# First modulation quarter in two eighths with three column groups in flight, and other orders on VectorE later on

## The reference, cut to what matters

```python
mod = jax.nn.silu(c) @ w_ada[l] + b_ada[l]
sh_m, sc_m, ga_m, sh_f, sc_f, ga_f = jnp.split(mod[:, None, :], N_MOD, axis=-1)
h = rmsnorm(x, g_pre_mix[l]) * (1.0 + sc_m) + sh_m
hq, hf, hi, hg, cq, ckv, kr, gate_a, gate_b = jnp.split(h @ w_in, split_idx, axis=-1)
...   # gated recurrence, latent attention, both projected; merged with sigmoid gates
x = x + ga_m * rmsnorm(y, g_post_mix[l])
h = rmsnorm(x, g_pre_ffn[l]) * (1.0 + sc_f) + sh_f
y = swiglu(h, w_gate_up[l], w_down[l])
x = x + ga_f * rmsnorm(y, g_post_ffn[l])
```

## Time and profile before

| what | value |
|---|---|
| median of the runs | 1868.36 us (1868.06, 1868.36, 2447.69) |
| the profiled execution's own time | 1869.41 us |
| its span | 1867.6 us |
| PE busy | 1820.3 us, 97% of the span |
| DVE busy | 1297.1 us, 69% |
| ACT busy | 894.0 us, 48% |
| moved by DMA | 423.38 MB, mean 227 GB/s |

### The profile page before, as it was taken

One profiled execution on the slowest core, in us unless ns is written; L12 is line 12 of the kernel. 1 busy time (PEld: TensorE's weight loads), 2 busy tenths in 40 slices (PEclk: granted clock), 3 DMA queues, 4 the chain that ended last, 5 costly groups with the idle time before them and its releaser, 6 DMA issues. The chain is left out here.

```text
span 1867.6 us, 24368 instructions
## 1 busy us (share of the span) xinstructions
PE 1820.3 (97%) x8828; PEld 1529.1 (82%) x8828; DVE 1297.1 (69%) x1373; ACT 894.0 (48%) x1023; POOL 105.1 (6%) x74
## 2 busy tenths in 40 slices
PE   3999999999999999999999999999999999999997
PEld 3878888888888888888888878888888888888886
DVE  6889768677677677668787555656666666665657
ACT  5544555645645645644444456443443443443343
POOL 0000000130130130130000000000000000000000
PEclk8999999999999999999999999999999999999999
DMA  9997547656656656547787645666666666665553
GB/s 360 402 385 270 190 169 279 227 175 220 226 175 218 230 171 219 202 158 244 282 324 242 225 158 193 221 231 221 206 235 225 212 224 225 224 212 176 195 188 128
DMA packets 115985, 423.38 MB, mean 227 GB/s; under 512 B 13008, under 2 KB 13392, under 8 KB 115408
## 3 DMA queue, kind: packets, MB, share of 16 engines
q1 hardware_dynamic: 115920, 422.51, 65.7%
HBM read 420.36 MB, written 2.10 MB: 226 GB/s over the span
## 5 line engine op out<-in xcount | busy, mean ns | idle before, releaser
L1320 DVE TENSOR_TENSOR wlo<-raw,whi 128x1024 fp32r<-128x1024 f32 x600 | 731.9, 1222 | 401.6 <-ACT whi L484 400.7
L484 ACT ACTIVATE whi<-raw 128x1024 fp32r<-128x1024 f32 x600 | 630.0, 1053 | 718.6 <-PE PS L898 660.4
L890 PE MATMUL PS<-whi,hT_hi 128*128 128x512 f32 x1760 | 694.4, 395 | 4.9 <-issue 3.0
L891 PE MATMUL PS<-whi,hT_lo 128*128 128x512 f32 x1760 | 686.5, 390 | 0.0
L898 PE MATMUL PS<-wlo,hT_hi 128*128 128x512 f32 x1760 | 471.4, 390 | 0.0
L890 PEld LDWEIGHTS PS<-whi,hT_hi 128*128 128x128 f32 x1760 | 331.2, 188 | 72.4 <-issue 3.3
L898 PEld LDWEIGHTS PS<-wlo,hT_hi 128*128 128x128 f32 x1760 | 330.8, 188 | 69.6
L891 PEld LDWEIGHTS PS<-whi,hT_lo 128*128 128x128 f32 x1760 | 331.3, 188 | 66.6 <-issue 0.2
L890 PE MATMUL PS<-whi,cT_hi 128*128 128x512 f32 (+1 forms) x592 | 229.4, 389 | 1.4 <-DVE side L1644 1.4
L891 PE MATMUL PS<-whi,cT_lo 128*128 128x512 f32 (+1 forms) x592 | 226.1, 384 | 0.0
L1327 DVE SCALAR_TENSOR_TENSOR ada_acc<-ada_raw,csilu,ada_acc 128x512 f32<-128x512 f32 (+1 forms) x185 | 141.2, 763 | 27.3 <-DMA ada_raw<-in_ada 23.4
(11 more groups left out here) (238 smaller groups left out, 1112.3 us busy)
## 6 DMA issues: line engine op xcount, KB each, us to landing
ada_raw<-in_ada SPq DMA_DIRECT2D x142, 512.0 KB, 4.8
raw<-in_w_gate SPq DMA_DIRECT2D x88, 512.0 KB, 4.1
raw<-in_w_up SPq DMA_DIRECT2D x88, 512.0 KB, 4.1
raw<-in_w_down SPq DMA_DIRECT2D x88, 512.0 KB, 4.1
raw<-in_w_start SPq DMA_DIRECT2D x80, 512.0 KB, 4.9
raw<-in_w_hf SPq DMA_DIRECT2D x32, 512.0 KB, 3.7
raw<-in_w_hq SPq DMA_DIRECT2D x32, 512.0 KB, 5.1
raw<-in_w_hi SPq DMA_DIRECT2D x32, 512.0 KB, 4.3
```

Of the source, the lines that this page charges most:

```text
L484: nc.scalar.activation(whi[:, pl.slot(c), 0:w], raw[:, pl.slot(c), 0:w], ACT.Copy)\
L890: nc.tensor.matmul(o, hi[:, kt, tok], whi[:, s, cols], start=c == 0 and k == 0, stop=False)
L891: nc.tensor.matmul(o, lo[:, kt, tok], whi[:, s, cols], start=False, stop=False)
L1320: nc.vector.tensor_tensor(wlo[:, s, 0:w], raw[:, s, 0:w], whi[:, s, 0:w].bitcast(F32), ALU.subtract)\
```

## The change

It has five parts.

1. **Eighths.** Slices 0 to 15 are cut otherwise on the host: the first eight hold all of the depth for the first eighth (256 rows of h, one chunk's depth), the next eight for the second. DVE takes each slice as two dependent instructions of 128x512 (`eighth_chunk`). Slices 1 and 3 are multiplied by PE (`shared_chunk`, 8 products with one column each), and PE's sum of the first eighth is laid on top.
2. **Three groups in flight.** With only the first eighth of h, PE multiplies the first chunk of groups 0, 1 and 2 (the third in banks 6 and 7), then the second chunk of each. The x transposes are spread between them.
3. **A later second quarter of modulation.** `ADA_PACE` takes 16 slices by chunk 19 instead of 15. For quarter 1 the sum moves behind the ninth group (ahead of chunk 18), the scale to chunk 20 on DVE, ACT's scaling to chunk 20, and the low part to chunk 21 on DVE. For quarters 2 and 3 these stand where they stood. `add_pair` goes ahead of the slice in DVE's loop.
4. **Later orders.** `T_OG` from 20 to 19. At the channel mixer's entry ACT takes `square_x2(0, ...)` ahead of `high(first, 1)`, and DVE takes each `h2_low` before the `low` or `mix_x2` that it followed.
5. **The end.** DVE no longer finishes token tile 0 before the last sums of tile 1: `add_rows(2, 1)` and `add_rows(3, 1)` stand between the output pieces of tile 0.

```diff
+ADA_SHARED = [1, 3]
+N_E = 3
-ADA_PACE = [(0, 0), (15, 16), (20, 21), (35, 32), (55, 48), (80, 48)]
+ADA_PACE = [(0, 0), (3, 2), (19, 16), (20, 17), (35, 32), (55, 48), (80, 48)]
...
+            return i * N_E + j if j < N_E else j * W_G + i
...
-            for a in range(KD):
+            for a in range(ADA_SLOTS):
                 load_ada0(a)
...
+            for c in range(N_E):
                 load(start, c, w_start[c])
+            for a in range(ADA_SLOTS, KD):
+                load_ada0(a)
+            load(start, N_E, w_start[N_E])
...
             high(pl, 0)
+            scale_rows(1, 0, 1)
             high(pl, 1)
-            scale_quarter(0)
+            copy_xT(2)
+            copy_xT(3)
+            high(pl, 2)
+            copy_xT(4)
+            copy_xT(5)
+            scale_rows(2, 1, 2)
+            copy_xT(6)
+            high(pl, N_E)
+            copy_xT(7)
...
-                if i == 17 and n < PH - 1:
-                    scale_quarter(n + 1)
+                for q, at in ((1, SG * W_G), (2, 2 * SG * W_G - 3), (3, 3 * SG * W_G - 3)):
+                    if c == at:
+                        scale_rows(q + 2, q * KP_Q, (q + 1) * KP_Q)
...
+            for a in ADA_SHARED:
+                shared_chunk(a)
+            pe.wait_ge(sig("constants_loaded"), 16)
+            pe.wait_ge(sig("x_scaled"), TT)
+            transpose_x(0)
+            transpose_x(1)
+            sum_first_eighth()
...
+            first_tile(0, 0)
+            transpose_x(4)
+            pe.wait_ge(sig("xT_copied"), 4)
+            first_tile(1, 0)
+            transpose_x(5)
+            first_tile(2, 0)
+            sum_second_eighth()
+            transpose_x(6)
+            first_tile(0, 1)
...
-                    if j == 6 and n < PH - 1:
+                    if j == (6 if n else 8) and n < PH - 1:
                         sum_quarter(n + 1)
...
+            second = [a for a in range(E_N, KD) if a not in ADA_SHARED]
+            eighth_chunk(second[0])
+            eighth_scale(0)
             low(pl, 0)
-            shift_and_scale(0)
-            quarter_low(0)
+            rows_low_start(0, 1)
+            eighth_chunk(second[1])
+            low(pl, 1)
+            eighth_chunk(second[2])
+            low(pl, 2)
+            for a in second[3:]:
+                eighth_chunk(a)
+            eighth_scale(1)
+            rows_low_start(1, 2)
+            low(pl, N_E)
...
+                for q, at in ((1, SG * W_G), (2, 2 * SG * W_G - 4), (3, 3 * SG * W_G - 4)):
+                    if c == at:
+                        quarter_scale(q)
+                for q, at in ((1, SG * W_G + 1), (2, 2 * SG * W_G - 2), (3, 3 * SG * W_G - 2)):
+                    if c == at:
+                        rows_low_start(q * KP_Q, (q + 1) * KP_Q)
...
-        T_CROSS, T_SUM, T_OG, T_OSQ, T_OMEAN, T_ON = DECAY[-1] - 2, DECAY[-1], 20, 21, 22, 24
+        T_CROSS, T_SUM, T_OG, T_OSQ, T_OMEAN, T_ON = DECAY[-1] - 2, DECAY[-1], 19, 21, 22, 24
...
+            add_rows(2, 0)
+            add_rows(3, 0)
+            y2_rms(0)
+            final(0, 0)
+            add_rows(2, 1)
+            final(1, 0)
+            final(2, 0)
+            add_rows(3, 1)
+            final(3, 0)
+            y2_rms(1)
+            for n in range(GD):
+                final(n, 1)
```

More of the change, by code:

```diff
@@ L389, in _ @@
                     ahead = KD + ada_due(c - RING + 1) + min(ADA_SLOTS, ADA_FIRST + (c - RING) // 3)
-                    for a in range(asked, min(ahead, ADA0)):
+                    for a in range(asked, min(ahead, ADA_ALL)):
                         load_ada0(a)
-                    asked = max(asked, min(ahead, ADA0))
+                    asked = max(asked, min(ahead, ADA_ALL))
                     if c == SG * W_G + RING:
@@ L776, in _ @@
             high(first, 0)
-            high(first, 1)
             square_x2(0, 0)
             square_x2(0, 1)
+            high(first, 1)
             square_out_rows(1)
@@ L1439, in _ @@
             tables()
-            for a in range(KD):
-                ada0_chunk(a)
+            for a in range(E_N):
+                if a not in ADA_SHARED:
+                    eighth_chunk(a)
                 if a == 2:
@@ L1504, in _ @@
             for c in range(N_C + AHEAD):
[L1505 removed]
+                if c > N_E:
                     low(pl, c)
                 n, i = divmod(c, SG * W_G)
[L1508 to L1513 removed]
                 j, odd = divmod(c - AHEAD, W_G)
@@ L1941, in _, with final, y2_rms @@
             gain_last(1)
-            for tt in range(TT):
-                for j in range(2, GD):
-                    add_rows(j, tt)
+            def final(n, tt):
+                cols = slice(n * NW, (n + 1) * NW)
+                dve.wait_ge(sig("y2_gained"), 2 * (tt + 1) + min(n - 1, 2) if n >= 2 else 2)
+                nc.vector.scalar_tensor_tensor(out=x2[:, tt, cols], in0=ya[:, tt, cols],
+                                               scalar=stat[:, 12 + tt:13 + tt], in1=x2[:, tt, cols],
+                                               op0=ALU.mult, op1=ALU.add).then_inc(sig("x_final"), 1)
+            def y2_rms(tt):
                 dve.wait_ge(sig("y2_squared"), 2 * TT + 2 * tt + 2)
```

194 lines of the change are left out of this document (125 added, 69 removed).

## The result

| kernel | median, us | lowest to highest | ratio to before, 95% interval |
|---|---|---|---|
| before | 1868.76 | 1868.06 to 1869.83 | |
| changed | 1881.98 | 1880.18 to 1882.39 | 1.0063, 1.0052 to 1.0074 |

The changed kernel is 13.2 us slower than before, where 1868.8 was forecast, and outside the range (1862 to 1873). By the 2% bound it is "no difference". Its profiled execution took 1881.98, its span is 1880.2. One execution of the kernel before, 2447.69 us, was in a slow state and is left out of the table.

What follows compares the result with a forecast made beforehand. PE bounds the kernel, busy 1820.3 of 1867.6 us. Terms: 2.7 later at chunk 28, -1.7 gate, -0.0 mixer's entry, -0.6 end, +0.4 on the profiled 1869.41; as a median 1868.8, range 1862 to 1873.

Steps and rivals of the forecast that it cites:

- Start: First chunks: PE begins chunk 0 at 28.2 instead of 39.95, chunk 3 at 45.2; a lead of 5.1 us.
- W: Time at which chunk 20 has landed: 84.7 by counted loads plus 4.3 us of pauses, 89.0.
- DVE keep up from chunk 4 on: Behind chunk 3: DVE needs 2.33 us for a chunk and a slice against PE's 2.72, so it keeps up.
- the same 4.3: Loads up to chunk 20: DMA pauses and lag add 4.3 us, as in the kernel before.
- The third rival: Slower (chance 0.2): DVE runs late after 46 us, DMA pauses repeatedly, W goes towards 94.1; total then 1873.9.
- The chain behind W: Boundary at chunk 20: rounding, scale, ACT's scaling and DVE's low part put PE's start at W + 12.3, 101.3.
- Half clock behind the wait: Chunk 20: PE's wait of 8 us drops the clock to half, costing 2.2 us.
- beyond it the order is that of before: After quarter 2's sum, covered by 1.9 us: the order is as before; only the later orders change the time.
- Later orders: Output gate -1.7 us, channel mixer's entry 0.0 (within 0.3 either way), the end -0.6.

Runs made afterwards that it cites:

- e1: The changed kernel with ACT's copy of x transpose 7 moved behind the rounding of chunk 6, no longer ahead of chunk 4's: 1876.37 us.
- e10: On top of e1, quarter 1's low part of h one place earlier on DVE, behind the low part of chunk 20 instead of 21: 1875.52 us.
- e13: The changed kernel with 43 idle products spread over waits PE has anyway, placing its recurrence loop elsewhere; ACT's copy left in place: 1874.39 us.
- e6: The kernel before with only the later orders: gate a step earlier, orders at the channel mixer's entry, and the end: 1864.79 us.
- e9: e1 with 43 idle products spread over waits that PE has anyway, placing its recurrence loop elsewhere: 1870.41 us.
- e15: The kernel before with 32 idle one-column products at PE's start, so that its loop begins 225 instructions behind a multiple of 256: 1869.09 us.
- e12: e6 with five idle products of 512 columns on PE, two ahead of the sum of quarter 0 and three behind it: 1865.61 us.
- e2: The changed kernel with its third part undone (pace of slices and quarter 1's sum, scale and low part as before the change): 1875.76 us.

## Why the prediction was wrong

- **Start.** Chunk 0 at 28.2, measured 28.41; chunk 3 at 45.2, measured 46.36. Right within 1.2 us. Behind it the sum took 2.72 us a chunk at once; chunk 3 ran at half clock and chunk 4 began 7.05 us after it, so PE came to its wait ahead of chunk 20 at 101.2, not at 93.3. That cost nothing, since chunk 20 hung on W.
- **The failed step: W, the landing of chunk 20.** The text has DVE keep up from chunk 4 on, and takes "the same 4.3" us of pauses from the kernel before. It did not follow ACT's queue behind chunk 3, where the last x copy waits for PE. The pauses came to 10.2 us (94.90 against 84.7). e1 takes the copy out and has W at 90.81; the 1.8 us to the forecast's 89.0 stay open. The third rival had this size, W at 94.1, but by DVE running late, not ACT.
- **The chain behind W.** 12.3 us forecast; 107.09 - 94.90 = 12.2 in the changed kernel, and 12.2 in e1. e10 shortened it to 8.2 (90.38 to 98.62), and chunk 20 came 4.4 earlier than in e1.
- **Half clock behind the wait.** 2.2 us forecast; chunk 20 took 5.07, 2.35 over. One more restart was not forecast, behind the sum ahead of chunk 18 (4.4 us for that chunk), though the wait ahead of it was only 0.33 us; it cost nothing, since PE waited for chunk 20 anyway. Chunk 28 is 8.5 us late where 2.7 were forecast, and the 5.9 of W are nearly the whole difference. That the clock fell was right; that it costs 2.2 was right within 0.2.
- **The second failed step: "beyond it the order is that of before".** True of the order, not of the place: 68 more instructions on PE put the recurrence's loop where its returns stall, a term of 7.2 us (7.6 by e13's median) that the sum did not have.
- **Later orders.** -2.3 forecast. The changed kernel's landmarks give -2.3 for the gate (forecast -1.7; three turns, 0.76 each), -0.2 at the mixer's entry (PE waits 1.68, 0.77 and 0.56 us where it had 2.22 and 1.60; forecast 0.0) and -0.6 at the end (as forecast); e6 gives -3.6.

The sum, by the landmarks of the two profiles: 8.5 us at chunk 28, 7.2 at the returns, less 2.3 for the gate and 0.8 for the mixer's entry and the end, is 12.6, the difference of the spans (1867.6 and 1880.2). The forecast had 2.7, nothing, -1.7 and -0.6; the 5.8 at chunk 28 and the 7.2 at the returns are what it lacked. With both mended, e9, the median is 1870.4. Of the 1.6 above the forecast, 1.2 are chunk 20, which e9 begins at 102.48 and the text at 101.3.

Not settled: why the body is loaded anew when a load is under way at the branch. That the two go together at all ten stalled returns and at no other is shown; what the sequencer does there is not.

## What to carry to other kernels

Follow every engine's queue past the point at which an order was changed until each instruction in it has its input, those with nobody waiting for them above all: here one such copy held three roundings, and through them the DMA. Count what a change adds to an engine's instructions ahead of a loop; if after it PE waits for "issue" at the loop's return, look whether instruction loads run through the loop's turns, and move the loop by padding inside waits before judging the change. And compare landmarks along the program, not totals: an equal total hid 5 us gained and 4 us lost.

## What the runs showed of the hardware

- A DMA queue loads PE's instructions, 16.3 KB at a time. A loop body of 1597 instructions ran its turns without a single load in twelve kernels (42 or 43 loads in all), with the body touching seven blocks of 256 and, in e15, eight. In five kernels (60 loads) a load was under way at the branch back; the body was loaded anew in each turn, nine loads, PE's sequencer spent 3.4 to 3.8 us on the branch, and PE stood 1.45 to 1.93 us.
- The clock fell to half behind a sum of 16 one-column products when a wait stood ahead of the sum: 1.52 us in e12 (fall at 35 us), 0.33 in the changed kernel (at 94), 1.62 in e2 (at 86). It did not behind one of 1.25 us in e10 (139.08), nor behind sums without a wait (80.30 before, 89.94 in e1). At the loop's returns it held behind a wait of 1.45 us in e1 and fell behind 1.70 in e10. So the length of the wait alone does not tell. The Trainium skill, "TensorE: Matmul & The Clock Gate", section "HAM oscillation — how this bites in real kernels", puts such falls down to waits between batches; these rows agree as to the wait of 5.88 us ahead of chunk 20.
- An idle float32 product of one column took 0.43 us at the start and 0.23 in e9 ahead of chunk 20 (36 matmuls in 4.08 us), and a wait that was already met 0.11 us per instruction on PE; neither is free padding.
